# Modulation row: a per-partition scalar multiply on Pool, the partition sum on PE ahead of b_in, and a 24 KB row stored and broadcast back

## The chip, the cores and the metric

The kernel runs on one core of a Trainium2 chip. The metric is the device time of one execution in microseconds; the median of three runs is given. The core has five engines: PE (matmul), DVE and ACT (elementwise work, both read PSUM), Pool (elementwise work in SBUF, and DMA issue), and SP, which here issues the weight loads.

## The reference, cut to what matters

The program is a stack of three transformer blocks at batch 1, 256 tokens, width 1024: a block with differential attention and a dense MLP, a block with a gated recurrence (`hgrn`) and a mixture of experts, and a second network with a modulated block. Only the last one uses the vector that this change is about:

```python
c_act = jax.nn.silu(c)                                   # (1, 1024)
ada = c_act @ w_ada[l] + b_ada[l]                        # (1, 6 * 1024)
shift_a, scale_a, gate_a, shift_m, scale_m, gate_m = jnp.split(ada, 6, axis=-1)
h = modulate(rmsnorm(x, g_mix[l]), shift_a, scale_a)     # h * (1 + scale) + shift
...
x = x + gate_a[:, None, :] * y
```

`ada` depends on `c`, `w_ada` and `b_ada` alone, so it can be computed at any time ahead of the second network. `w_ada` is 1024 x 6144 in float32, 24 MB.

## The kernel before, in words

The stages run one after another, in the order kv_a, kv_b, a_in, diff, a_mem, a_out, dense, b_in, hgrn, b_mem, b_out, route, experts, ada, in_2, gla, moba, out_2, ff_2, final. Every engine has its own instruction list in that order, and semaphores are written out by hand (`wait_ge`, `then_inc`); `at(label)` is the semaphore and count that a labelled instruction sets.

Weight products: SP fills a ring of six 1 MB units (`raw`). For each unit ACT rounds it to a high part (`w_hi`, L787), DVE takes the remainder (`w_lo`, L1183), both with two buffers, and PE forms three products: high by high (L1803), high weight by low activation (L1804), low weight by high activation (L1811). `turn_split` transposes the 256 x 1024 activation on PE (L1828), and ACT (L807) and DVE (L1221) split it into `hT_hi` and `hT_lo`. In `turn_split` and `product` of a stage, each engine works strictly in order.

The modulation vector is built by Pool during dense and b_in, in `ada_sums` (L451 to L488). It keeps six rows of 1024 columns per partition (`acc`, in `work`). For each of the 8 blocks of 128 input rows and each of the 6 parts of 1024 columns, it loads 512 KB of `w_ada` (L465, three buffers, two rows ahead), multiplies it by the column `c_col` (L476), and adds it to `acc` (L479): 48 rounds. After them the partial sums of all 128 partitions, 3 MB, go to DRAM (`ada_parts`, L488), because the buffer `work` is written in stage hgrn. ACT and DVE wait for that store (`ada_stored`, L977 and L1505) ahead of their first instruction of hgrn.

After the experts Pool reads the 3 MB back into `ada` in three DMAs (L736). PE sums over the partitions with a matrix of ones (`ones`, L2171), 12 matmuls of 512 columns, which leaves the sum in all partitions; ACT copies the 12 results back to `ada` (`ada_out`, L921), six ahead of the squares of `norm_2` and six behind them. DVE needs `ada` in `norm` at L1197 (scale) and L1215 (shift), and the gain row `g_mix`, which Pool loads behind the three reads (L689).

In hgrn, PE transposes the outputs of b_in (`turn("hgrn_q", ...)`, L1828), ACT copies them out (L813), DVE clears buffers (L1347) and then runs the recurrence, with Pool's `tree_keys` (L501).

Of the kernel before, what the change touches and what calls it, by code (L numbers as in the profile page):

```python
# [142 lines left out]
def program(nc, A, consts, buckets, out, semaphores, numbers, known, stages, capacity):  # L143
# [17 lines left out]
    with ctx:  # L161
# [16 lines left out]
        c_col = sb("c_col", [P, KC])  # L178
        sumsq = sb("sumsq", [P, TILES])
# [52 lines left out]
        ada_parts = nc.dram_tensor("ada_parts", (P, N_ADA * D), F32, kind="Internal").ap()  # L232
# [47 lines left out]
        def have(name):  # L280
            return name in stages
# [168 lines left out]

        def ada_sums(pool):  # L451
# [16 lines left out]
            def row_block(k, last):  # L468
                for a in range(N_ADA):
# [6 lines left out]
                    pool.tensor_tensor(row, row, c_col[:, k:k + 1].broadcast_to([P, D]), ALU.mult).then_inc(ada_scaled, 1)  # L476
# [10 lines left out]
            pool.wait_ge(ada_ready, N_ADA * (KC + 1))  # L487
            pool.dma_start(ada_parts, work[:, 0:N_ADA * D]).then_inc(ada_stored, 16)  # L488
# [186 lines left out]
        def _(pool):  # L675
# [18 lines left out]
            pool.memset(ones[:, :], 1.0)  # L694
            pool.memset(zero[:, :], 0.0).then_inc(S("zero"), 1)
# [35 lines left out]
            if have("ada"):  # L731
# [3 lines left out]
                for n in range(N_ADA // 2):  # L735
                    pool.dma_start(ada[:, 2 * n:2 * n + 2, :].rearrange("p a d -> p (a d)"),  # L736
                                   ada_parts[:, 2 * n * D:(2 * n + 2) * D]).then_inc(ada_back[n], 16)
# [36 lines left out]
        def _(act):  # L774
# [142 lines left out]
            def ada_out(first, end):  # L917

                for j in range(first, end):
                    act.wait_ge(*at("ada", "summed", j))  # L920
                    act.activation(ada[:, j // 2, j % 2 * 512:(j % 2 + 1) * 512], bank[j % 6][:, :], ACT.Copy)\  # L921
                       .then_inc(S("ada", "out", j), 1)

# [44 lines left out]
            if have("b_in"):  # L968
# [3 lines left out]
                turn_split("norm_b", G["b_in"])  # L972
                product("b_in", proj)
            if have("hgrn"):
                S.stage("hgrn")
                if have("ada"):
                    act.wait_ge(ada_stored, 16)  # L977
# [113 lines left out]
            if have("ada"):  # L1091
                S.stage("ada")
                norm("norm_final", x, mix, at("experts done"))
                ada_out(0, 6)
            if have("in_2"):
                norm("norm_2", x, mix, at("norm_final", "h"))
                ada_out(6, 12)
# [71 lines left out]
        def _(dve):  # L1169
# [332 lines left out]
            if have("hgrn"):  # L1502
                S.stage("hgrn")
                if have("ada"):
                    dve.wait_ge(ada_stored, 16)  # L1505
# [206 lines left out]
            if have("ada"):  # L1712
                S.stage("ada")
                norm("norm_final", x, x, 8)
                dve.wait_ge(*at("ada", "out", 3))
            if have("in_2"):
                S.stage("in_2")
                norm("norm_2", x, mix, 9, 0)
                dve.wait_ge(*at("ada", "out", 11))
# [70 lines left out]
        def _(pe):  # L1790
# [230 lines left out]
            if have("b_in"):  # L2021
                S.stage("b_in")
                turn_split("norm_b", mix, at("norm_b", "h"))
                product("b_in", "norm_b")
# [139 lines left out]
            if have("ada"):  # L2164
                S.stage("ada")
# [117 lines left out]
```

## Time and profile before

| | |
|---|---|
| median of 3 runs | 2169.84 us (2169.73 to 2171.62) |
| span of the profiled execution | 2169.8 us |
| PE busy | 1929.8 us (89%) |
| DVE busy | 1500.8 us (69%) |
| ACT busy | 1140.2 us (53%) |
| Pool busy | 373.6 us (17%) |
| HBM read | 513.72 MB, 239 GB/s over the span |

The profile is of one execution. Its span is the median of the timed runs to within 0.1 us, so times read in it can be set against the median directly. The page gives busy times per engine, the busy share in 40 slices, and the chain of work that ended last: from the last instruction back, at each step to what released it. The trace behind it answers for one stretch, one line or one engine. By the page's slices of 54 us, Pool is busy for 90% or more of the time from about 217 to 488 us.

### The profile page before, as it was taken

Reading aid. Unit: us, or ns where it says so; the run is one execution under the profiler, and the core shown is the slowest. Engines: PE = TensorE matmul, PEld = TensorE weight load, DVE = VectorE, ACT = ScalarE, POOL = GpSimd, SP = SyncE. Lnnn points to the kernel's source line nnn. Section 1 sums busy time; section 2 is a strip of 40 time slices with the busy share of each in tenths; the row PEclk is TensorE's granted clock in tenths of the full one; section 3 lists DMA queues with packets and bytes.
Section 4 is the critical chain, followed back from the end, with each engine's and each line's share of the span. In section 5 each row is a group of like instructions: output and inputs, shape, how many; then the busy total and the mean of one; then the engine's idle time right before and its main releaser. Section 6 shows DMA issues by size and latency. Waiting matters only on the chain.

```text
span 2169.8 us, 27789 instructions
## 1 busy us (share of the span) xinstructions
PE 1929.8 (89%) x9182; PEld 1604.5 (74%) x9182; DVE 1500.8 (69%) x1230; ACT 1140.2 (53%) x1136; POOL 373.6 (17%) x212
## 2 busy tenths in 40 slices
PE   6967899795677999999999999999999798779995
PEld 4856688685666887878788787878878567668894
DVE  4454667573853989879798887988888642645554
ACT  5344334342033767767676676767767553234331
POOL 1005999995400000000000000000000000300000
PEclk9987899897875999999999999999999888679998
DMA  8504678675022999999999999999999843225540
GB/s 290 204 1 144 215 255 259 213 240 177 1 78 64 353 366 320 366 307 365 336 346 369 305 366 312 363 338 343 366 307 367 311 140 116 59 78 173 176 155 20
DMA packets 357365, 518.68 MB, mean 239 GB/s; under 512 B 17106, under 2 KB 286578, under 8 KB 356672
## 3 DMA queue, kind: packets, MB, share of 16 engines
q1 hardware_dynamic: 346736, 476.24, 65.0%
q0 software_dynamic: 10576, 41.76, 5.8%
q8 instruction: 30, 0.49, 0.1%
q14 instruction: 23, 0.19, 0.0%
HBM read 513.72 MB, written 4.21 MB: 239 GB/s over the span
## 4 chain that ended last, share of the span: by engine, by line
PE 69%; POOL 13%; DVE 8%; ACT 4%; issue 4%; DMA 1%; DVEq 0%; ACTq 0%; POOLq 0%
PE bank L1803 20%; PE bank L1811 20%; PE bank L1804 19%; POOL work L479 7%; POOL work L476 6%; PE bank L1878 2%; PE bank L2089 1%; PE bank L1828 1%; DVE w_lo L1183 1%; PE bank L2074 1%; PE bank L1915 1%; ACT w_hi L787 1%; PE bank L1893 1%; PE bank L2050 1%; DVE plain L1372 1%
## 5 line engine op out<-in xcount | busy, mean ns | idle before, releaser
L1183 DVE TENSOR_TENSOR w_lo<-raw,w_hi 128x2048 fp32r<-128x2048 f32 (+1 forms) x454 | 1086.4, 2397 | 190.1 <-ACT w_hi L787 171.2
L787 ACT ACTIVATE w_hi<-raw 128x2048 fp32r<-128x2048 f32 (+1 forms) x454 | 865.9, 1911 | 592.6 <-PE bank L1804 548.8
L1803 PE MATMUL bank<-w_hi,slot_hi 128*128 128x512 f32 x896 | 365.9, 408 | 0.0
L1804 PE MATMUL bank<-w_hi,slot_lo 128*128 128x512 f32 x896 | 354.5, 396 | 0.0
L1803 PE MATMUL bank<-w_hi,hT_hi 128*128 128x512 f32 (+2 forms) x864 | 305.7, 367 | 4.0 <-ACT w_hi L787 4.0
L1804 PE MATMUL bank<-w_hi,hT_lo 128*128 128x512 f32 (+2 forms) x864 | 302.2, 363 | 0.0
L1803 PE MATMUL bank<-w_hi,hid_hi 128*128 128x512 f32 x664 | 261.8, 394 | 6.8 <-DVE hid_lo L1603 4.2
L1804 PE MATMUL bank<-w_hi,hid_lo 128*128 128x512 f32 x664 | 260.2, 392 | 0.0
L1811 PE MATMUL bank<-w_lo,slot_hi 128*128 128x512 f32 x896 | 243.2, 393 | 0.3
L1811 PEld LDWEIGHTS bank<-w_lo,slot_hi 128*128 128x128 f32 x896 | 168.6, 189 | 38.4 <-DVE w_lo L1183 2.4
L1803 PEld LDWEIGHTS bank<-w_hi,slot_hi 128*128 128x128 f32 x896 | 170.7, 191 | 34.0 <-issue 0.3
L1804 PEld LDWEIGHTS bank<-w_hi,slot_lo 128*128 128x128 f32 x896 | 171.2, 191 | 32.8
L1803 PEld LDWEIGHTS bank<-w_hi,hT_hi 128*128 128x128 f32 x864 | 169.9, 197 | 29.3 <-issue 2.9
L1811 PE MATMUL bank<-w_lo,hid_hi 128*128 128x512 f32 x664 | 177.3, 396 | 12.7 <-DVE w_lo L1183 12.7
L1804 PEld LDWEIGHTS bank<-w_hi,hT_lo 128*128 128x128 f32 x864 | 169.5, 196 | 23.8
L736 POOL DMA_DIRECT2D ada<-ada_parts x3 | 1.6, 528 | 1074.1 <-DVE headsq L1711 1074.1
L1811 PE MATMUL bank<-w_lo,hT_hi 128*128 128x512 f32 (+2 forms) x864 | 181.7, 356 | 0.3 <-DVE w_lo L1183 0.3
L1811 PEld LDWEIGHTS bank<-w_lo,hT_hi 128*128 128x128 f32 x864 | 145.4, 192 | 23.5 <-DVE w_lo L1183 1.1
L1811 PEld LDWEIGHTS bank<-w_lo,hid_hi 128*128 128x128 f32 x664 | 124.4, 189 | 41.8 <-DVE w_lo L1183 15.7
L479 POOL TENSOR_TENSOR work<-work 128x1024 f32<-128x1024 f32 x48 | 151.2, 3150 | 4.0
L1803 PEld LDWEIGHTS bank<-w_hi,hid_hi 128*128 128x128 f32 x664 | 124.8, 188 | 35.3 <-issue 3.6
L1804 PEld LDWEIGHTS bank<-w_hi,hid_lo 128*128 128x128 f32 x664 | 124.9, 188 | 26.4
(258 smaller groups left out, 1676.6 us busy)
## 6 DMA issues: line engine op xcount, KB each, us to landing
raw<-in_moe_w_gate_up SPq DMA_DIRECT2D x448, 512.0 KB, 6.1
raw<-in_moe_w_down SPq DMA_DIRECT2D x224, 512.0 KB, 5.5
raw<-in_w_ff SPq DMA_DIRECT2D x64, 512.0 KB, 4.3
work<-in_w_ada POOLq DMA_DIRECT2D x48, 512.0 KB, 4.3
raw<-in_dense_w_gate_up SPq DMA_DIRECT2D x44, 512.0 KB, 5.3
raw<-in_b_w_in SPq DMA_DIRECT2D x24, 512.0 KB, 5.1
raw<-in_w_in SPq DMA_DIRECT2D x24, 512.0 KB, 4.7
raw<-in_dense_w_down SPq DMA_DIRECT2D x22, 512.0 KB, 5.0
```

What stands on the lines that cost most here:

```text
L476: pool.tensor_tensor(row, row, c_col[:, k:k + 1].broadcast_to([P, D]), ALU.mult).then_inc(ada_scaled, 1)
L479: pool.tensor_tensor(acc[:, a, :], acc[:, a, :], row, ALU.add).then_inc(ada_ready, 1)
L787: act.activation(w_hi[:, g % SPLIT, 0:n], raw[:, g % RING, 0:n], ACT.Copy).then_inc(R.hi, 1)
L1183: dve.tensor_tensor(w_lo[:, g % SPLIT, 0:n], raw[:, g % RING, 0:n], f32(w_hi[:, g % SPLIT, 0:n]), ALU.subtract).then_inc(R.lo, 1)
L1372: dve.tensor_tensor(dq, d.q, d.after, ALU.mult).then_inc(S(tag, "queries", level), 1)
L1803: pe.matmul(out_, hi, w_hi[:, s, c:c + w], start=(start and n == 0), stop=False, skip_group_check=True)
L1804: mm = pe.matmul(out_, lo, w_hi[:, s, c:c + w], start=False, stop=False, skip_group_check=True)
L1811: mm = pe.matmul(out_, hi, w_lo[:, s, c:c + w], start=False, stop=(stop and n == len(terms) - 1), skip_group_check=True)
L1828: mm = pe.transpose(bank[6 + j % 2][:, c * P:(c + 1) * P], b, ident)
L1878: mm = pe.matmul(bank[6 + k][:, j * a.dv:(j + 1) * a.dv], a.probsT[k][:, m, s, t * P:(t + 1) * P], a.v(i, m, s), start=(s == 0), stop=(s = ...
L1893: mm = pe.transpose(bank[4 + m][:, s * SEQ + t * P:s * SEQ + (t + 1) * P], a.probs[i % 2][:, m, t, s * P:(s + 1) * P], ident)
L1915: mm = pe.matmul(bank[3 * (level % 2) + n // 4][:, n % 4 * P:(n % 4 + 1) * P], dk[r, h // d.per, c], dq[r, h // d.per, c], start=True, sto ...
```

## The change

Four things change.

- In `row_block`, Pool's multiply becomes `tensor_scalar` with the per-partition scalar `c_col[:, k:k + 1]` where it was `tensor_tensor` with that column broadcast over 1024 elements.
- Ahead of the transposes of b_in, PE waits for the last addition of `ada_sums` and sums the 12 pieces of 512 columns over the partitions: the weights are 12 columns of `one_row`, zero but for the one column that picks the output row, so 12 matmuls accumulate into 12 partitions of `bank[0]`. ACT copies that 12 x 512 block to `work` (`ada_place`) behind its part of `turn_split`, and PE waits for that copy ahead of the product of b_in, which writes the same bank.
- Pool stores this block, 24 KB, in place of the 3 MB, once ACT has copied it. ACT and DVE no longer wait for the store ahead of hgrn.
- After the experts Pool's three reads broadcast the 24 KB to all partitions of `ada`. The 12 matmuls with `ones` and the 12 copies go away; DVE waits for the reads (`ada_back`) itself.

```diff
--- before.py
+++ after.py
@@ -176,6 +176,7 @@
         zero = sb("zero", [P, P], BF16)
         ones = sb("ones", [P, P])
         c_col = sb("c_col", [P, KC])
+        one_row = sb("one_row", [P, 4 * N_ADA - 1])
         sumsq = sb("sumsq", [P, TILES])
         rstd = sb("rstd", [P, TILES])
         top = sb("top", [P, 2, 4])
@@ -229,7 +230,7 @@
         over.close()
 
         bank = [ctx.enter_context(nc.psum_tensor(f"bank{i}", [P, 512], F32)) for i in range(8)]
-        ada_parts = nc.dram_tensor("ada_parts", (P, N_ADA * D), F32, kind="Internal").ap()
+        ada_dram = nc.dram_tensor("ada_dram", (2 * N_ADA, 512), F32, kind="Internal").ap()
         rel_rows = nc.dram_tensor("rel_rows", (2 * MOBA_PAIRS, 2 * SEQ), F32, kind="Internal").ap()
 
 
@@ -448,6 +449,10 @@
         more_loop = ExpertLoop("more")
         ff_loop = Loop("ff")
 
+        def ada_place():
+
+            return work[0:2 * N_ADA, 9216:9728]
+
         def ada_sums(pool):
 
 
@@ -473,7 +478,7 @@
                         load_row(k, ahead)
                     pool.wait_ge(ada_in[a % ADA_BUFFERS], 32 * k + 16 * (a // ADA_BUFFERS + 1))
                     row = rows[:, a % ADA_BUFFERS, :]
-                    pool.tensor_tensor(row, row, c_col[:, k:k + 1].broadcast_to([P, D]), ALU.mult).then_inc(ada_scaled, 1)
+                    pool.tensor_scalar(row, row, c_col[:, k:k + 1], None, ALU.mult).then_inc(ada_scaled, 1)
                     pool.wait_ge(ada_scaled, N_ADA * k + a + 1)
                     pool.wait_ge(ada_ready, N_ADA * k + a + 1)
                     pool.tensor_tensor(acc[:, a, :], acc[:, a, :], row, ALU.add).then_inc(ada_ready, 1)
@@ -484,8 +489,8 @@
             pool.wait_ge(*at("ada", "c"))
             for k in range(KC):
                 row_block(k, k == KC - 1)
-            pool.wait_ge(ada_ready, N_ADA * (KC + 1))
-            pool.dma_start(ada_parts, work[:, 0:N_ADA * D]).then_inc(ada_stored, 16)
+            pool.wait_ge(*at("ada", "row"))
+            pool.dma_start(ada_dram, ada_place()).then_inc(ada_stored, 16)
 
         def tree_keys(pool, S, tag):
 
@@ -692,6 +697,9 @@
             load_gain()
             load_gain()
             pool.memset(ones[:, :], 1.0)
+            pool.memset(one_row[:, 0:2 * N_ADA - 1], 0.0)
+            pool.memset(one_row[:, 2 * N_ADA:], 0.0)
+            pool.memset(one_row[:, 2 * N_ADA - 1:2 * N_ADA], 1.0)
             pool.memset(zero[:, :], 0.0).then_inc(S("zero"), 1)
             if have("a_in"):
                 load_gain()
@@ -734,7 +742,8 @@
                 pool.wait_ge(ada_stored, 16)
                 for n in range(N_ADA // 2):
                     pool.dma_start(ada[:, 2 * n:2 * n + 2, :].rearrange("p a d -> p (a d)"),
-                                   ada_parts[:, 2 * n * D:(2 * n + 2) * D]).then_inc(ada_back[n], 16)
+                                   ada_dram[4 * n:4 * n + 4, :].rearrange("a d -> (a d)").partition_broadcast(P))\
+                        .then_inc(ada_back[n], 16)
                 pool.dma_start(w_gate[:, :], A["w_gla_gate_2"][0]).then_inc(loaded["wgate"], 16)
             if have("in_2"):
                 load_gain()
@@ -913,13 +922,6 @@
                     split_hi(R, g + 5, rounds)
                     silu(1)
                     hidden_hi(1)
-
-            def ada_out(first, end):
-
-                for j in range(first, end):
-                    act.wait_ge(*at("ada", "summed", j))
-                    act.activation(ada[:, j // 2, j % 2 * 512:(j % 2 + 1) * 512], bank[j % 6][:, :], ACT.Copy)\
-                       .then_inc(S("ada", "out", j), 1)
 
             def prepare():
 
@@ -970,11 +972,12 @@
                 begin("b_in")
                 norm("norm_b", x, mix, [at("dense", "added", t) for t in range(TILES)])
                 turn_split("norm_b", G["b_in"])
+                if have("ada"):
+                    act.wait_ge(*at("ada", "summed"))
+                    act.activation(ada_place(), bank[0][0:2 * N_ADA, :], ACT.Copy).then_inc(S("ada", "row"), 1)
                 product("b_in", proj)
             if have("hgrn"):
                 S.stage("hgrn")
-                if have("ada"):
-                    act.wait_ge(ada_stored, 16)
                 turn_copy("hgrn_q", flat(hgrn.q), HG_W * TILES)
 
                 for n in range(HG_W * TILES // 512):
@@ -1091,10 +1094,8 @@
             if have("ada"):
                 S.stage("ada")
                 norm("norm_final", x, mix, at("experts done"))
-                ada_out(0, 6)
             if have("in_2"):
                 norm("norm_2", x, mix, at("norm_final", "h"))
-                ada_out(6, 12)
                 S.stage("in_2")
                 begin("in_2")
                 turn_split("norm_2", G["in_2"])
@@ -1501,8 +1502,6 @@
                 product("b_in", False)
             if have("hgrn"):
                 S.stage("hgrn")
-                if have("ada"):
-                    dve.wait_ge(ada_stored, 16)
                 decayed_start(hgrn)
                 dve.wait_ge(*at("hgrn_f", "taken", 2))
                 low, high = (lb[:, n, :].unsqueeze(2).broadcast_to([P, HG_HEADS, SEQ]) for n in (2, 3))
@@ -1712,11 +1711,12 @@
             if have("ada"):
                 S.stage("ada")
                 norm("norm_final", x, x, 8)
-                dve.wait_ge(*at("ada", "out", 3))
+                dve.wait_ge(ada_back[0], 16)
             if have("in_2"):
                 S.stage("in_2")
                 norm("norm_2", x, mix, 9, 0)
-                dve.wait_ge(*at("ada", "out", 11))
+                for n in (1, 2):
+                    dve.wait_ge(ada_back[n], 16)
                 turn_split("norm_2")
                 product("in_2", False)
                 split_lo(ring, G["in_2"] + 12, 0, KC * GLA_RANK)
@@ -2020,7 +2020,15 @@
                        lambda i: mlp_round(ring, dense_loop, G["dense"] + 3, i, 2 * i + 1, TILES, 2, model_xs))
             if have("b_in"):
                 S.stage("b_in")
+                if have("ada"):
+                    pe.wait_ge(ada_ready, N_ADA * (KC + 1))
+                    for j in range(2 * N_ADA):
+                        mm = pe.matmul(bank[0][0:2 * N_ADA, :], one_row[:, 2 * N_ADA - 1 - j:4 * N_ADA - 1 - j],
+                                       work[:, j * 512:(j + 1) * 512], start=(j == 0), stop=(j == 2 * N_ADA - 1))
+                    mm.then_inc(S("ada", "summed"), 1)
                 turn_split("norm_b", mix, at("norm_b", "h"))
+                if have("ada"):
+                    pe.wait_ge(*at("ada", "row"))
                 product("b_in", "norm_b")
             if have("hgrn"):
                 S.stage("hgrn")
@@ -2161,19 +2169,9 @@
                     pe.sem_inc(more_ring.hi_used, RING)
                     pe.sem_inc(more_ring.used, RING)
                     experts(more_ring, more_loop)
-            if have("ada"):
-                S.stage("ada")
-                pe.wait_ge(*at("experts done"))
-                for j in range(2 * N_ADA):
-                    pe.wait_ge(ada_back[j // 4], 16)
-                    if j >= 6:
-                        pe.wait_ge(*at("ada", "out", j - 6))
-                    pe.matmul(bank[j % 6][:, :], ones[:, :], ada[:, j // 2, j % 2 * 512:(j % 2 + 1) * 512], start=True, stop=True)\
-                      .then_inc(S("ada", "summed", j), 1)
             if have("in_2"):
                 S.stage("in_2")
                 turn_split("norm_2", mix, at("norm_2", "h"))
-                pe.wait_ge(*at("ada", "out", 11))
                 product("in_2", "norm_2")
                 b = B["in_2"] + 6
                 pe.wait_ge(block_out, b - 2)
```

## Rows read from the trace of the kernel before

**Rows 1.** The page's chain that ended last, by engine, share of the span.
```profile
PE 69%; POOL 13%; DVE 8%; ACT 4%; issue 4%; DMA 1%; DVEq 0%; ACTq 0%; POOLq 0%
```

**Rows 2.** Who waited for whom, 500 to 560 us: total us, times, longest us.
```profile
DVE work L1347 <- DMA ada_parts<-work: 22.8, 1, 22.8
ACT work L813 <- DMA ada_parts<-work: 18.2, 1, 18.2
```

**Rows 3.** The chain in order of time, 500 to 545 us: start us, us, what.
```profile
516.79 9.34 DMA ada_parts<-work
...
526.15 0.60 ACT work L813
```

**Rows 4.** Pool in order of time: start us, us, line, operation.
```profile
195.36 1.89 POOL L476 TENSOR_TENSOR work<-work,c_col 128x1024 f32<-128x1024 f32 x1 [1.37 <-DMA work<-in_w_ada]
...
416.30 1.91 POOL L476 TENSOR_TENSOR work<-work,c_col 128x1024 f32<-128x1024 f32 x1
418.29 2.35 POOL L479 TENSOR_TENSOR work<-work 128x1024 f32<-128x1024 f32 x1
...
421.55 1.90 POOL L476 TENSOR_TENSOR work<-work,c_col 128x1024 f32<-128x1024 f32 x1
...
514.15 2.34 POOL L479 TENSOR_TENSOR work<-work 128x1024 f32<-128x1024 f32 x1
```

**Rows 5.** Pool's groups, shapes kept apart: busy us, mean ns | idle before.
```profile
L479 POOL TENSOR_TENSOR work<-work 128x1024 f32<-128x1024 f32 x48 | 151.2, 3150 | 4.0
L476 POOL TENSOR_TENSOR work<-work,c_col 128x1024 f32<-128x1024 f32 x48 | 125.3, 2610 | 2.1 <-DMA work<-in_w_ada 1.4
...
L459 POOL MEMSET work<- 128x1024 f32 x6 | 5.4, 946 | 16.9 <-DVE mix L1298 16.9
```

**Rows 6.** Pool and DVE in order of time, within dense.
```profile
319.56 4.33 POOL L479 TENSOR_TENSOR work<-work 128x1024 f32<-128x1024 f32 x1
...
322.52 3.52 DVE L1183 TENSOR_TENSOR w_lo<-raw,w_hi 128x2048 fp32r<-128x2048 f32 x1 [0.89 <-ACT w_hi L787]
...
324.80 3.00 POOL L476 TENSOR_TENSOR work<-work,c_col 128x1024 f32<-128x1024 f32 x1
```

**Rows 7.** PE in order of time, from the head to the end of b_in.
```profile
429.84 1.97 PE L1828 MATMUL bank<-con,mix 128*128 128x128 f32 x8 [11.35 <-DVE mix L1204]
...
434.05 0.78 PE L1803 MATMUL bank<-w_hi,hT_hi 128*128 128x512 f32 x1
...
507.99 1.10 PE L1828 MATMUL bank<-con,proj 128*128 128x128 f32 x8 [0.75 <-ACT proj L828]
```

**Rows 8.** ACT in order of time, its last split piece ahead of b_in.
```profile
434.43 0.60 ACT L807 ACTIVATE hT_hi<-bank 128x512 fp32r<-128x512 f32 x1 [0.26 <-PE bank L1828]
```

**Rows 9.** Stretches: us, busy PE, PEld, DVE, ACT, POOL, PEclk, DMA, GB/s.
```profile
434.00:440.00 6.00, 6.00 (x20) 4.80 (x19) 5.63 (x4) 0.89 (x3) 5.60 (x4) 0.67 0.37 113
500.00:508.00 8.00, 7.25 (x56) 6.82 (x54) 2.15 (x1) 2.57 (x5) 7.52 (x6) 1.00 0.96 309
```

**Rows 10.** All engines in order of time, after the experts.
```profile
1727.44 1.57 POOL L736 DMA_DIRECT2D ada<-ada_parts  x3 [1074.11 <-DVE headsq L1711]
...
1731.18 2.48 DVE L1204 SCALAR_TENSOR_TENSOR x<-x,rstd,gain 128x1024 f32<-128x1024 f32 x2
1732.88 13.31 PE L2171 MATMUL bank<-ada,ones 128*128 128x512 f32 x24 [9.91 <-DMA ada<-ada_parts]
...
1741.57 1.05 ACT L797 ACTIVATE mix<-x 128x1024 f32<-128x1024 f32 x1
...
1743.93 1.22 DVE L1197 SCALAR_TENSOR_TENSOR ada<-ada,gain 128x1024 f32<-128x1024 f32 x1
...
1747.77 2.36 DVE L1215 TENSOR_TENSOR mix<-mix,ada 128x1024 f32<-128x1024 f32 x2
```

**Rows 11.** The g_mix load: its issue, then size and us to landing.
```profile
1729.50 0.55 POOL L689 DMA_DIRECT2D gain<-in_g_mix  x1
...
gain<-in_g_mix POOLq DMA_DIRECT2D x1, 512.0 KB, 9.6
```

## The prediction

> **What bounds the kernel now.** I read the page's chain first: PE carries 69% of it, but Pool carries 13% [rows 1], though Pool is busy for 17% of the span. So there is a stretch in which the Pool loop that builds the modulation vector is itself the bound. The waits around the end of b_in show where: ACT stands 18.2 us and DVE 22.8 us for the store of `ada_parts` [rows 2]. The chain in order of time puts it together: Pool's last addition starts at 514.15 [rows 4] and ends at 516.5, the 3 MB store takes 9.34 us, and hgrn begins at 526.15 [rows 3]. PE had begun hgrn's transposes at 507.99 [rows 7]. The first four of them are half of 1.10 us, and ACT could have copied them out at about 508.7. So 17.5 us lie between what b_in allows and what Pool and its store allow. This is the gain on offer at this place. From 434.05 to 507.99 [rows 7] PE is at work on the product of b_in; that stretch is PE's, not Pool's.
>
> **The sum goes by one time, P, at which Pool finishes its last addition.** Before, P is 516.5, and nothing on PE depends on it: PE starts b_in at 429.84 [rows 7]. After, PE waits for P ahead of b_in. Everything of b_in is queued behind that wait: PE's transposes, hence ACT's and DVE's halves of `turn_split`, which wait for them in order, and the weight splits behind these; the ring then fills and SP stops too. So the store leaves the path behind P (9.3 us), and the whole of b_in, some 80 us, moves from beside Pool to behind P. That is worth it only if P comes down to about where PE wants to start.
>
> **How far P comes down.** A round without disturbance takes 421.55 less 416.30, 5.25 us: 1.91 for the multiply, 2.35 for the addition, and 0.99 of issue, descriptors and small gaps [rows 4]. Over the 48 rounds the means are 2.61 and 3.15 [rows 5], so a round takes 6.75 us, of which 1.50 is waiting. The rows of both engines show what for [rows 6]: the addition of 319.56 takes 4.33, `w_lo` on DVE, issued during it, takes 3.52 instead of about 2.3 and ends at 326.0, and the multiply of 324.80 takes 3.00 instead of 1.91. They take turns: each stands while the other runs. The Trainium skill (SBUF — State Buffer, "Who interferes with whom") says that a DVE instruction with two SBUF inputs contends with a GpSimd instruction that reads SBUF; the trace agrees (4.33 against 2.35 us), and by it the new multiply, which still reads SBUF, goes on colliding.
>
> The trace has no `tensor_scalar` of this size on Pool. From below, the memset of the same 1024 columns, one stream out and none in, takes 0.946 us [rows 5]; from above, the present multiply takes 1.91 us [rows 4]; nothing excludes that the new form is as slow as that one, and nothing in it is less work than a memset. I take 1.0: with a single full stream in, beside one out, it is nearer to the memset, which has no second operand to fetch. The skill (GPSIMD Engine Reference, "Engine selection") calls one-input operations on GpSimd roughly line-rate; at its 1.2 GHz that is an estimate of 0.85 us, with which the sum below would come out 8 us lower. The same page (§3.1) also gives 1.8 cycles an element as the best of a tight loop, 1.54 us, an estimate with which the sum would be some 25 us higher. No row here decides between them.
>
> With 1.0 a round without waiting is 4.34 us. The waiting I scale with the length of the round, since `w_lo` comes at PE's pace: 1.50 x 5.6 / 6.75 = 1.25, together 5.59. From the first multiply at 195.36 [rows 4] to 429.8 that is 41.9 rounds. From there on PE stands, and DVE with it (its `turn_split` waits for PE), so the other 6.1 rounds take 4.34 us, 26.4 us. The last two rounds load nothing and save the 0.9 us between 420.64 and 421.55 each. P = 429.8 + 26.4 - 1.8 = 454.5, say 455.
>
> **From P to the start of hgrn.** The 12 matmuls: their moving operand has 512 columns of float32, as that of L2171, of which 12 take 13.31 us from an idle PE [rows 10] (two records each). PE will have been idle as there, so I take 13.3. The 12-column weights change nothing that I can price: bounds are 10.3 (all at the late pace) and 20.5 (all at the early pace of 1.71 us). Then the transposes. Before, 4.2 us lay between their start and the product's [rows 7]. Now PE is at full clock, where eight take 1.10 instead of 1.97 us [rows 7]; but PE waits for ACT's copy of the row, and ACT makes it behind its four split pieces. The fourth starts 4.6 us after the first transpose and takes 0.60 [rows 8]; about 1 us less for the faster transposes, one more copy of about 0.65: 4.9 us. Then the product: 434.05 to 508.7 before, 74.65 us, less 1.8 us because the first 6 us ran at a granted clock of 0.67 [rows 9], now full: 72.85. With 0.05 for the semaphore, hgrn starts at P + 91.1. For P = 455 that is 546.1, against 526.15: 19.95 us later.
>
> **After the experts.** Removed are 12 matmuls (13.31 us, of which the first six lie ahead of ACT's squares) and 12 ACT copies. The squares of `norm_2` started at 1741.57 because six copies stood ahead of them; they need only `norm_final`, done at 1733.66 [rows 10]. The next thing is late instead: L1197 needs the gain `g_mix`, issued by Pool behind the three reads at 1729.50 and landed 9.6 us later, 1739.1 [rows 11]. L1197 started at 1743.93 [rows 10], so 4.8 us are gained; 7.8 would be without that load. The broadcast reads write the same 3 MB into SBUF as the reads they replace, so I leave their time as it is; the first is needed at 1736, the others by 1746, and issued at 1727.44 to 1728.5 they fit. If they read slower, the gain of this part is gone: 0 is its other bound. PE starts in_2 from idle both times.
>
> **At nothing:** three memsets of `one_row` at the start (no longer than the 1.0 of a 1024-column one together, and Pool's next load waits for a used gain buffer there); Pool's new wait for the row ahead of its store (behind it only the load of `b_out_norm` and `tree_keys`, both for hgrn, 70 us later); the 24 KB store (needed after the experts). The waits of ACT and DVE ahead of hgrn that disappear are the 9.3 us already counted.
>
> **Sum:** 19.95 - 4.8 = +15.2 us. The span of the profile, 2169.8, is the median to 0.1 us, so 2169.8 + 15.2 = 2185 us. The sum changes sign at P = 439.9, where Pool would have to be 15 us faster than I expect.
>
> **Rivals.**
> - *The multiply gets little or nothing from the new form* (Pool spends its time on something other than the second operand). At 1.91 us a round stays 6.75: 34.7 rounds by 429.8, the other 13.3 at 5.25 less 1.8, P = 498, +58 us, 2228. At 1.4 us P is 474.5, +35, 2204. For it: a column broadcast as second operand already costs 0.44 less than a full one (1.91 against 2.35), so half of it may be gone. Against: the memset's 0.946. Chance of 1.5 us or more: 0.18.
> - *Collisions fall by more than the length of a round*, because a shorter multiply seldom holds DVE back, and so DVE seldom stands in front of the addition. Half the waiting, 0.75 a round: 5.09 us, 46.0 rounds by 429.8, P = 436.5, -3.4 us, 2166.4: no change. Chance 0.12. For it: the 4.33 additions come where DVE was already queued.
> - *Faster: Pool is done before PE needs it.* One mechanism: multiply at the memset's 0.95 and waiting down to a third, 0.5: 4.79 us a round, P = 195.4 + 48 x 4.79 - 1.8 = 423.5, and the 12 matmuls run while PE would be idle for `norm_b` (it is idle for 11.35 us there [rows 7]). The path then has the matmuls' last part only: hgrn some 10 us earlier, and 4.8 behind: -15, 2155. It decides at P under 435.5. Against it: the addition alone, which stays, waits 0.8 a round. Chance 0.08.
> - My own case, P from 444 (0.95 us, 1.0 of waiting) to 476: 2174 to 2206. Chance 0.62.
>
> A difference of 0.2%, 4.3 us, is about what a measurement of this kernel can tell from none. Faster by more: 0.08; within: 0.12; slower by more: 0.80. The range leaves out the faster case, half of the unchanged one, and the multiply above 1.6 us: 2168 to 2216.
>
> **What would show it.** In the changed profile: the mean of the new multiply (1.0, with collisions 1.5) and of the addition (3.0); Pool's last addition at 455; a wait of PE of about 36 us for Pool ahead of the 12 matmuls, at a granted clock of 0.5 at first; no wait of ACT or DVE for a store at hgrn; hgrn's first copy at 546; a DVE wait for the DMA of `g_mix` at L1197. Wrong would be a Pool that ends before 440, or a b_in product that is more than 3 us off 72.

## The result and the profile after

The changed kernel takes 2268.74 us (median; 2267.57 to 2269.20) against 2169.78 before: ratio 1.0446, 95% interval 1.0431 to 1.0462. The direction was forecast, the size was not: 2185 was expected, with 2216 as the upper end.

The head of the page, after:

```profile
span 2265.8 us, 27773 instructions
...
PE 1942.2 (86%) x9182; PEld 1597.9 (71%) x9182; DVE 1469.2 (65%) x1230; ACT 1133.8 (50%) x1125; POOL 378.7 (17%) x215
...
PE 70%; POOL 13%; DVE 8%; issue 4%; ACT 3%; DMA 1%; DVEq 0%; ACTq 0%; POOLq 0%
```

The shares of the chain hardly differ from [rows 1]: Pool is on it for 13% both times, though of a longer span. Pool's two groups over the whole execution (busy us, mean ns | idle before), and then single instructions late in the loop (start us, us):

```profile
L481 POOL TENSOR_SCALAR work<-work,c_col 128x1024 f32<-128x1024 f32 x48 | 155.9, 3249 | 3.2 <-DMA work<-in_w_ada 1.4
L484 POOL TENSOR_TENSOR work<-work 128x1024 f32<-128x1024 f32 x48 | 124.8, 2601 | 4.3
```

```profile
481.66 2.85 POOL L481 TENSOR_SCALAR work<-work,c_col 128x1024 f32<-128x1024 f32 x1
484.60 2.33 POOL L484 TENSOR_TENSOR work<-work 128x1024 f32<-128x1024 f32 x1
...
487.88 2.85 POOL L481 TENSOR_SCALAR work<-work,c_col 128x1024 f32<-128x1024 f32 x1
...
519.93 2.34 POOL L484 TENSOR_TENSOR work<-work 128x1024 f32<-128x1024 f32 x1
```

The new multiply takes 2.85 us undisturbed, where the old one took 1.91 [rows 4] and I had taken 1.0. A round beside an idle DVE takes 6.22 us (487.88 less 481.66). Pool ends at 522.3, 5.8 us later than before, and PE now waits for it. Who waited for whom between 400 and 680 us (total us, times, longest us), and PE and ACT behind that wait (start us, us):

```profile
ACT hT_hi L816 <- PE bank L1828: 110.9, 2, 110.0
DVE hT_lo L1222 <- ACT hT_hi L816: 108.6, 2, 107.8
...
PE bank L2026 <- POOL work L484: 101.8, 1, 101.8
```

```profile
522.32 13.01 PE L2026 MATMUL bank<-work,one_row 128*12 128x512 f32 x24 [101.80 <-POOL work L484]
535.26 1.09 PE L1828 MATMUL bank<-con,mix 128*128 128x128 f32 x8
...
539.17 0.57 ACT L977 ACTIVATE work<-bank 12x512 f32<-12x512 f32 x1
...
612.55 1.08 ACT L822 ACTIVATE work<-bank 128x512 f32<-128x512 f32 x2 [0.75 <-PE bank L1828]
```

The last line is hgrn's first copy, which came at 526.15 before [rows 3]. The two waits for the store [rows 2] are gone, and a wait of 101.8 us of PE has come instead. After the experts (DVE, start us, us):

```profile
1834.35 0.17 DVE L1194 TENSOR_SCALAR sumsq<-sumsq 128x2 f32<-128x2 f32 x1 [2.32 <-ACT mix L806]
1837.19 1.22 DVE L1198 SCALAR_TENSOR_TENSOR ada<-ada,gain 128x1024 f32<-128x1024 f32 x1 [2.67 <-DMA gain<-in_g_mix]
```

This is the wait for the gain row. From the end of the experts (`headsq`, 1727.07 before and 1825.44 after) to PE's first transpose of in_2 it is 23.1 us before and 18.0 after.

The two profiled spans differ by 96.0 us. They divide at two marks into 86.4 us up to hgrn's first copy (612.55 less 526.15), 12.0 us from there to the end of the experts (1212.9 against 1200.9), and -2.4 us behind it (440.4 against 442.7). The second part was in no step of the prediction. The medians differ by 99.0 us. In every other run here the time of the profiled execution is 1.8 us above its span, so that of before is the one timed at 2171.62, and that its span equals the median is a coincidence.

### The profile page after: what moved, and what is told of

Same layout as the page of the kernel before. It is cut to its first block, busy times and chain, and to the rows that moved or that the text cites. A ratio compares the mean times of both kernels' runs of the same rounds, so it can differ in the third digit from the quotient of the medians.

```text
span 2265.8 us, 27773 instructions
## 1 busy us (share of the span) xinstructions
PE 1942.2 (86%) x9182; PEld 1597.9 (71%) x9182; DVE 1469.2 (65%) x1230; ACT 1133.8 (50%) x1125; POOL 378.7 (17%) x215
## 4 chain that ended last, share of the span: by engine, by line
PE 70%; POOL 13%; DVE 8%; issue 4%; ACT 3%; DMA 1%; DVEq 0%; ACTq 0%; POOLq 0%
PE bank L1803 20%; PE bank L1804 20%; PE bank L1811 20%; POOL work L481 7%; POOL work L484 6%; PE bank L1828 1%; PE bank L2097 1%; PE bank L1878 1%; PE bank L2082 1%; DVE w_lo L1184 1%; PE bank L1915 1%; PE bank L2058 1%; PE bank L2026 1%; PE bank L1893 1%; DVE top L1275 1%
## 5 line engine op out<-in xcount | busy, mean ns | idle before, releaser
L1184 DVE TENSOR_TENSOR w_lo<-raw,w_hi 128x2048 fp32r<-128x2048 f32 (+1 forms) x454 | 1055.8, 2329 | 221.5 <-ACT w_hi L796 208.9
L481 POOL TENSOR_SCALAR work<-work,c_col 128x1024 f32<-128x1024 f32 x48 | 155.9, 3249 | 3.2 <-DMA work<-in_w_ada 1.4
```

What stands on the lines that cost most here:

```text
L481: pool.tensor_scalar(row, row, c_col[:, k:k + 1], None, ALU.mult).then_inc(ada_scaled, 1)
L1184: dve.tensor_tensor(w_lo[:, g % SPLIT, 0:n], raw[:, g % RING, 0:n], f32(w_hi[:, g % SPLIT, 0:n]), ALU.subtract).then_inc(R.lo, 1)
```

## The experiments

Two questions: is the first part the price of the multiply and the place of the wait, and nothing else; and where do the 12 us come from. Each ratio is against the kernel before on the same chip. Where a time has no ratio with it, it is of one run; 17 runs of before on one chip took 2165.26 to 2175.52 us, so a single time tells little below 5 us, and the rows of the trace tell more.

**The multiply alone, the arrangement alone.** In `ts_only` the kernel before gets the new multiply; in `tt_multiply` the changed kernel gets the old one back. The lines are those of `tt_multiply`; `ts_only` has them the other way round.

```diff
-                    pool.tensor_scalar(row, row, c_col[:, k:k + 1], None, ALU.mult)
+                    pool.tensor_tensor(row, row, c_col[:, k:k + 1].broadcast_to([P, D]), ALU.mult)
```

> The kernel before with nothing changed but the multiply, which becomes the one with a per-partition scalar. Theory: it takes 2.85 us undisturbed wherever it stands, 0.94 more than the old form, and waits less (0.96 us a round against 1.5 in dense), so a round takes about 7.15 us: Pool ends at 195.4 + 48 x 7.15 - 1.8 = 537, the store lands at 546.5, 20 us later than before: 2190 us. Rival: its 2.85 us belong to the changed kernel only (place of the buffers, or Pool running alone); then it takes no more than 1.91 here and the time is 2170 or less.

> The changed kernel with the multiply of before (column broadcast, two operands); all else as changed. Theory: of the loss, what is due to the multiply's form goes, and what is due to PE waiting ahead of b_in stays. A multiply alone takes 1.91 us again, 35 rounds are done by 429.8 us as before, the other 13 run beside an idle DVE at 5.25 us less 1.8: Pool ends at about 497.5. hgrn's first copy comes 90.3 us behind that, as it does in the changed kernel (522.3 to 612.6), so at 588, 61.6 us later than before, and 5.1 us are gained after the experts: 2226 us. Rival: the multiply's form is not what costs; then Pool ends near 522 again and the time stays near 2268.

`ts_only` took 2191.02 us, ratio 1.0105 (1.0075 to 1.0136), as expected. One multiply in it beside an idle DVE, the waits between 400 and 680 us, and hgrn's first copy:

```profile
514.88 2.85 POOL L476 TENSOR_SCALAR work<-work,c_col 128x1024 f32<-128x1024 f32 x1
```

```profile
DVE work L1347 <- DMA ada_parts<-work: 44.3, 1, 44.3
...
ACT work L813 <- DMA ada_parts<-work: 38.9, 1, 38.9
```

```profile
546.54 1.09 ACT L813 ACTIVATE work<-bank 128x512 f32<-128x512 f32 x2 [38.88 <-DMA ada_parts<-work]
```

So the multiply costs the same 2.85 us in either kernel, and here Pool ends at 536.8 and hgrn starts 20.4 us later than before. `tt_multiply` took 2245.53 us, 1.035 (1.0327 to 1.0372). hgrn's first copy was expected at 588:

```profile
588.76 1.08 ACT L822 ACTIVATE work<-bank 128x512 f32<-128x512 f32 x2 [0.75 <-PE bank L1828]
```

Pool ends at 498.9. The arrangement with the old multiply, that is PE's wait for Pool ahead of b_in less the store that it saves, costs 62.6 us at this mark. The time on the whole missed its expectation by 19 us, because the 12 us are in this kernel too (1212.5 us from that copy to the end of the experts). Of the rest, 4.9 us lie behind the experts, 0.8 ahead of hgrn, and 1.8 are the step from a span to a time.

**What the new multiply is made of.** `ts_imm` has the number 1.0 where the column stood; `ts_512` multiplies only half the columns.

```diff
-                    pool.tensor_scalar(row, row, c_col[:, k:k + 1], None, ALU.mult)
+                    pool.tensor_scalar(row, row, 1.0, None, ALU.mult)                                   # ts_imm
+                    pool.tensor_scalar(row[:, 0:512], row[:, 0:512], c_col[:, k:k + 1], None, ALU.mult) # ts_512
```

> The changed kernel with the immediate 1.0 as the scalar in place of the column (the factor c is left out of the modulation vector, nothing else). It asks what the 2.85 us are made of. If they come from fetching the scalar of each partition, the multiply falls to about 1.0 us, Pool ends at about 455 and the time is about 2185, the blind sum with its own price. If they belong to the form itself, the multiply stays at 2.85 and the time near 2268.

> The changed kernel with the new multiply on the first 512 of each 1024 columns only (the other half of each row is added unscaled). It gives the slope of the new multiply. Theory: 2.85 us for 1024 columns is nearly all per column, 2.7 ns each, with 0.1 fixed, so 512 take 1.45 us. Rival: the form has a fixed cost of about 1.9 us above a line-rate multiply; then 512 columns take about 2.4 us. With 1.45 us a round is 4.8 us undisturbed, Pool ends near 478, and the time is about 2268.7 - 44 = 2225; with 2.4 us near 2248.

They took 2266.45 and 2230.49 us, one run each; the second is 5 us above its expectation. One multiply of each, beside an idle DVE:

```profile
512.16 2.77 POOL L481 TENSOR_SCALAR work<-work 128x1024 f32<-128x1024 f32 x1
```

```profile
452.11 1.57 POOL L481 TENSOR_SCALAR work<-work,c_col 128x512 f32<-128x512 f32 x1
```

The column as scalar, in place of a number, is 0.08 us of it. Between 512 and 1024 columns the time goes from 1.57 to 2.85: 2.5 ns a column, and by that slope 0.29 us fixed (1.45 us was expected for 512). The form itself is slow per column on Pool: 2.5 ns, where the two-operand multiply with a broadcast column takes 1.91 us for 1024, under 1.9 ns a column. Why it is so, no run shows.

**What the arrangement gives when Pool is early.**

```diff
-            for k in range(KC):
-                row_block(k, k == KC - 1)
+            for k in range(KC // 2):
+                row_block(k, k == KC // 2 - 1)
...
-                    pe.wait_ge(ada_ready, N_ADA * (KC + 1))
+                    pe.wait_ge(ada_ready, N_ADA * (KC // 2 + 1))
```

It also has the old multiply, as `tt_multiply`.

> The changed kernel with the old multiply and only 4 of the 8 blocks of w_ada (24 of 48 rounds; the other half of the sum is left out), so that Pool is done long before PE reaches b_in. It shows what the arrangement gives when its condition holds. Theory: Pool ends at 195.4 + 24 x 6.75 - 1.8 = 356; the 12 matmuls run while PE waits for norm_b and end at 432; hgrn's first copy comes at about 511 where it came at 526, and 5.1 us are gained after the experts; with the 12 us lost in between as in the others, 2161 us. Rival: the wait ahead of b_in costs for another reason than Pool's lateness; then hgrn starts later than 526 here too.

It took 2167.64 us in one run. PE and ACT in it:

```profile
422.66 10.47 PE L2026 MATMUL bank<-work,one_row 128*12 128x512 f32 x24
433.06 1.09 PE L1828 MATMUL bank<-con,mix 128*128 128x128 f32 x8
```

```profile
511.81 1.09 ACT L822 ACTIVATE work<-bank 128x512 f32<-128x512 f32 x2 [0.74 <-PE bank L1828]
```

With Pool done in time (at 360.0), PE does not wait, and hgrn starts 14.3 us earlier than before, 0.8 us from what was expected. The 12 matmuls take 10.47 us here against 13.01: the granted clock is 1.00 from 420 to 435 us in this run, and 0.80 over the 13 us of the matmuls in the changed kernel. The whole time is 6.6 us above its expectation; 3.1 of them lie behind the experts (440.7 us, where 437.6 were expected), 1.8 are the step from span to time.

**The sum behind b_in.** The old multiply, and the wait moved to where `work` is needed. Not shown: the sum ahead of b_in goes away, ACT's copy of the row moves behind the product, and DVE waits for the sum ahead of hgrn.

```diff
                 turn_split("norm_b", mix, at("norm_b", "h"))
-                if have("ada"):
-                    pe.wait_ge(*at("ada", "row"))
                 product("b_in", "norm_b")
             if have("hgrn"):
...
+                    pe.wait_ge(*all_in)
+                    for j in range(2 * N_ADA):
+                        pe.wait_ge(ada_ready, N_ADA * KC + j // 2 + 1)
+                        mm = pe.matmul(bank[0][0:2 * N_ADA, :], one_row[:, 2 * N_ADA - 1 - j:4 * N_ADA - 1 - j],
...
```

> The old multiply, and the sum over the partitions moved from ahead of b_in to behind its product: each of the 12 matmuls waits only for its own part of the vector, and ACT and DVE wait for the sum ahead of hgrn. Theory: it is the place of the wait that costs, so b_in is beside Pool again, Pool ends at 516.5 as before, ten of the matmuls run beside Pool's last rounds, two behind it (3.4 us at the low clock), then the 12-partition copy: hgrn's first copy at 521.3, 5 us earlier than before, and 5.1 us are gained after the experts: 2160 us. Rival: the matmuls or the 12-partition copy cost more than the 9.3 us store they replace, wherever they stand; then hgrn starts later than 526 and the time is 2165 or more.

It took 2177.64 us, 1.0043 (1.0031 to 1.0056): neither 2160 nor a gain. But hgrn's first copy came early enough:

```profile
512.40 10.47 PE L2034 MATMUL bank<-work,one_row 128*12 128x512 f32 x24 [0.75 <-ACT proj L837]
...
522.80 1.10 PE L1830 MATMUL bank<-con,proj 128*128 128x128 f32 x8
```

The copy is at 523.5, 2.65 us earlier than before. Pool ended at 519.4 and was not the limit. The matmuls were: they run in a row behind the product, where I had expected ten of them beside Pool's last rounds. The loss is again behind that mark: 1212.8 us to the end of the experts, against 1200.9 before.

**The 12 us.** The cast of `pickT` happens once in each of the eight experts, so its first and last start bound seven steps. In before the first step takes 151.6 us and the other six 127.8 to 129.0. This view of one tile (durations ns min/median/max, first and last start us) for before, after, `late_sum`, and `ts_only`:

```profile
L1636 DVE CAST pickT<-staged x8: 279/286/295, 694.9 to 1618.2; 128x256 fp32r<-128x256 f32 x8
```

```profile
L1635 DVE CAST pickT<-staged x8: 282/284/293, 780.8 to 1714.4; 128x256 fp32r<-128x256 f32 x8
```

```profile
L1637 DVE CAST pickT<-staged x8: 280/282/294, 691.1 to 1624.8; 128x256 fp32r<-128x256 f32 x8
```

```profile
L1636 DVE CAST pickT<-staged x8: 279/282/294, 717.7 to 1640.9; 128x256 fp32r<-128x256 f32 x8
```

Seven steps take 923.3, 933.6, 933.7 and 923.2 us. The kernels with `one_row` are 10 us slower here, though the experts' code is the same. `one_row` is a new buffer ahead of the large ones (`proj`, `work`, `hid`, `slot`): 23 columns, 92 bytes a partition, which I take as rounded up to 96. `raw`, `w_hi`, `w_lo`, `hT_hi` and `hT_lo` are allocated ahead of it and do not move. Eight kernels vary that alone:

```diff
+        one_row = sb("one_row", [P, 4 * N_ADA - 1])   # row_only: the kernel before, buffer and memsets, unused
+        one_row = sb("one_row", [P, 32])              # row_32; 16, 64, 128 columns in row_16, row_64, row_128
-        one_row = sb("one_row", [P, 4 * N_ADA - 1])   # the kernels with PE's sum:
+        one_row = sb("one_row", [P, 64])              # late_sum_64, after_64
```

> The kernel before with only the 23-column buffer one_row added behind c_col, and its three memsets; nobody reads it. In the changed kernel and in both variants with PE's sum, an expert takes 129.7 us where it takes 128.6 before and in the kernel with the new multiply alone, and the whole stretch from hgrn's first copy to the end of the experts is 12 us longer. Theory A: the 92 bytes a partition move every later buffer (slot_hi, hid_hi, proj and so on) off a 64-byte boundary, and PE's matmuls from them get 1% slower; then this kernel shows 129.7 us an expert and some 10 us on the whole, 2179. Theory B: it is the altered instruction list of PE (its loops lie at other places in memory); then this kernel is like before, 128.6 us an expert, 2168.

> The kernel with the sum behind b_in's product, with one_row 64 columns wide (256 bytes a partition) instead of 23 (92 bytes), which leaves the later buffers at the same place modulo 64 bytes as before. Theory A (buffer places): an expert takes 128.6 us again and the 12 us go: 2177.6 - 12 = 2166, under the kernel before. Theory B (PE's instruction list): an expert stays at 129.7 and the time near 2177.

> The changed kernel with one_row 64 columns wide instead of 23, nothing else. It splits the loss of 99 us into its two causes. Theory: the wait ahead of b_in stays as it is (Pool ends at about 522, hgrn's first copy near 612.6), and the 12 us of buffers off a 64-byte boundary go: an expert takes 128.6 us, the whole 2268.7 - 12 = 2257. Rival: the 12 us came with the late start of the stages, and stay: 2268.

> The control for row_only: the kernel before with the same unused buffer and memsets, but 32 columns (128 bytes a partition), which moves the later buffers by two times 64 bytes. Theory: it is the place modulo 64 bytes that costs, so this kernel is as before, an expert 128.6 us, ratio 1.000. Rival: any shift, or the memsets, cost; then it is at 1.0067 as row_only.

> The kernel before with an unused buffer of 64 columns (256 bytes a partition) behind c_col and its three memsets. Theory (place of the later buffers modulo 256 bytes): as before, 128.6 us an expert, ratio 1.000. Rival (the memsets or the altered Pool list): 129.8 us and 1.007, as with 23 and 32 columns.

> The same with 128 columns (512 bytes). Theory: 128.6 us an expert, as before. Rival (only one particular place is fast): 129.8.

> The same with 16 columns (64 bytes). Theory: 129.8 us an expert and some 12 us on the whole, since 64 is no multiple of 256. Rival (the place modulo 64 matters after all, and row_32 was slow for another reason): 128.6.

> The kernel before with two unused buffers of 32 columns, one behind c_col and one ahead of proj: the small buffers in between (sumsq to flag) move by 128 bytes, proj, work, hid, slot and all behind them by 256. Theory: the large ones, from which PE reads its weights in dense and experts, have to keep their place, so 128.6 us an expert. Rival: the small ones do, and it stays at 129.8.

I take the large buffers to begin at byte 158784 of a partition before, which is 64 modulo 256. No view of a run shows an address, so the third column rests on that; the shifts in the second do not. Steps from the same view as above, of one profiled execution each:

| kernel | shift, bytes | place modulo 256 | seven steps, us | ratio (interval), or one run |
|---|---|---|---|---|
| before | 0 | 64 | 923.3 | |
| row_64 | 256 | 64 | 923.5 | 1.0003 (0.9988 to 1.0019) |
| row_128 | 512 | 64 | 923.4 | 2169.51 us |
| row_small | 256 (small ones 128) | 64 | 923.4 | 2174.11 us |
| late_sum_64 | 256 | 64 | 923.6 | 0.9958 (0.9940 to 0.9976) |
| after_64 | 256 | 64 | 921.1 | 1.0368 (1.0350 to 1.0385) |
| row_16 | 64 | 128 | 917.0 | 2166.22 us |
| row_only | 96 | 160 | 933.6 | 1.0067 (1.0044 to 1.0090) |
| row_32 | 128 | 192 | 933.8 | 1.0071 (1.0057 to 1.0086) |

`row_only` and `late_sum_64` settled that the place of the buffers is the cause and not PE's instruction list: an unused buffer brings the loss, and 256 bytes instead of 96 take it away. My first rule, modulo 64 bytes, fell with `row_32`: its buffers are at a multiple of 64 and it is slow. Modulo 256 fits the nine. `row_16` missed its expectation: 64 bytes of shift are not slow but faster than before. In `row_small` the small buffers move by 128 bytes and the large ones by 256, and its steps are those of before: the place of the large ones matters, and the shift of the small ones costs nothing. `after_64` gained more than expected: its first copy of hgrn comes at 617.7 (612.6 was expected, Pool ends at 527.0), but 1198.6 us lie from there to the end of the experts and 433.8 behind them, where the changed kernel has 1212.9 and 440.4.

What is slower is each matmul that reads a moved buffer. In dense, the streamed operand `w_hi` is the same for two kinds of matmuls: those that load `hT_hi` and `hT_lo` as their other operand (LDWEIGHTS), which did not move, and those that load `hid_hi` and `hid_lo`, which did. The first and last start of a run of both kinds, in `row_32` and then in before (start us, us):

```profile
301.81 0.39 PE L1808 MATMUL bank<-w_hi,hT_lo 128*128 128x512 f32 x1
...
305.01 0.39 PE L1808 MATMUL bank<-w_hi,hT_lo 128*128 128x512 f32 x1
...
307.05 0.40 PE L1807 MATMUL bank<-w_hi,hid_hi 128*128 128x512 f32 x1
...
310.55 0.40 PE L1808 MATMUL bank<-w_hi,hid_lo 128*128 128x512 f32 x1
```

```profile
300.04 0.40 PE L1804 MATMUL bank<-w_hi,hT_lo 128*128 128x512 f32 x1
...
303.26 0.39 PE L1804 MATMUL bank<-w_hi,hT_lo 128*128 128x512 f32 x1
...
305.30 0.39 PE L1803 MATMUL bank<-w_hi,hid_hi 128*128 128x512 f32 x1
...
308.73 0.40 PE L1804 MATMUL bank<-w_hi,hid_lo 128*128 128x512 f32 x1
```

These are 14 and 15 steps: 229 ns from start to start with `hT` and 233 with `hid` in `row_32`, 230 and 229 in before. Over the whole execution, the median from one start to the next behind a matmul of `w_hi` with `hT_hi` is 227 ns in all of these kernels. With `hid_hi` it is 229 in before, 227 in `row_16`, 232 in `row_only` and 236 in `row_32`. In the last six of the seven steps PE is busy for 98% of the time (758.83 of 771.7 us in before, 764.08 of 779.0 in `row_32`), so a per cent of its work is a per cent of the time.

**A version that beats both.** `late_sum_64` with the load of `g_mix` ahead of the three reads, and then the same with two other places of the large buffers:

```diff
                 load_gain()
+                if have("in_2"):
+                    load_gain()
                 pool.wait_ge(*at("experts done"))
```

> late_sum_64 with the load of the gain row g_mix issued before the three reads of the modulation row instead of behind them. Theory: in the changed kernel the scale step of norm_2 waits for that load (landed at 1837.2, where the squares were done at about 1834.5); with it away the first read becomes the limit or the squares do, and 2.7 us are gained against late_sum_64. Rival: the first read of the row lands no earlier than the gain did, and nothing is gained.

> late_gain_64 with one_row 80 columns wide (320 bytes), so that the large buffers begin at 128 modulo 256 where they began at 64. Theory: 127.8 us an expert as in row_16, 6.5 us less over the seven steps between experts, and 7 us on the whole: about 0.988 of before where late_gain_64 has 0.991. Rival: the gain of row_16 belonged to that kernel; then 128.6 and 0.991.

> The same with 48 columns (192 bytes), so that the large buffers begin at a multiple of 256 bytes. Theory: this is the natural boundary and at least as good as 128, so 127.8 us an expert or less, 0.988. Rival: the pace does not follow the boundary; then anything up to 129.9 us an expert and 0.997.

`late_gain_64` took 2155.27 us, 0.9911 (0.9883 to 0.9939). From the end of the experts to L1198 it is 9.0 us, with the squares as the limit:

```profile
1732.20 0.17 DVE L1194 TENSOR_SCALAR sumsq<-sumsq 128x2 f32<-128x2 f32 x1 [2.33 <-ACT mix L806]
1732.27 1.22 DVE L1198 SCALAR_TENSOR_TENSOR ada<-ada,gain 128x1024 f32<-128x1024 f32 x1
```

In `late_sum_64` it was 11.7 us, with a wait of 2.58 us for the gain: 2.7 us as expected. `late_gain_80` (place 128) took 2148.48 us, 0.9898 (0.9881 to 0.9916), with 919.7 us for the seven steps; its interval overlaps that of `late_gain_64`, so the steps show the better place and the whole time does not. `late_gain_48` (place 0) had 930.5 us for the seven steps and a ratio of 0.9995 (0.9982 to 1.0007): the multiple of 256 bytes is not the good place. Its profiled execution, 2163.02 us, is the fastest of its 12 runs (2163.02 to 2174.26).

## Why the prediction was right or wrong

**What bounds the kernel, and the sum by P: right.** The blind sum said that hgrn's first copy comes at P + 91.1. It came at P + 90.3 in the changed kernel, P + 89.9 with the old multiply. The parts held too: the 12 matmuls 13.01 us against 13.3, the product of b_in 72.75 us (539.80 to 612.55) against 72.85, a granted clock of 0.52 while PE waits for Pool (421 to 522 us), no wait for a store at hgrn.

**The price of the multiply: wrong, and most of the miss.** I put it between the memset's 0.946 and the old multiply's 1.91 us, took 1.0, and named nothing that would make it slower than the form that it replaces. It takes 2.85. The upper end was no bound: a row of another form says what that form costs, not that the new one can't cost more, and that the new form has one operand less to fetch was an argument about the work, not about how Pool does it. With 2.85 and the waiting left at 1.25, the same steps give 31.5 rounds by 429.8 and 16.5 more at 6.19, less 1.8: P = 530, 75 us above the forecast. With the measured waiting they give what was measured: 33 rounds by 429.8, 15 more at 6.22, less 1.8, is 521.3 against 522.3. So the price of the multiply put P 75 us off, and the smaller waiting took 8 us back. The Trainium skill (GPSIMD Engine Reference, "Engine selection") has one-input operations on GpSimd at roughly line-rate. This case's trace disagrees, with 2.5 ns a column for this one, which at the 1.2 GHz of that page is an estimate of three cycles; the measurement decides.

**The waiting of a round: wrong in size, to the other side.** I scaled it to 1.25 us. In the changed kernel it was 0.96 up to 429.8 (means of 3.43 and 2.72 us against 2.85 and 2.34 undisturbed), with a longer round. The rival that collisions fall with a shorter multiply had its reason wrong as well: the waiting fell, from 1.55 in the same stretch of before, with a longer one.

**The rivals.** "The multiply gets little or nothing from the new form" was the right kind of rival, at a chance of 0.18 and a price of 58 us, cut off at the old duration; beyond it lay what happened. The faster and the unchanged rival need P under 440. `half_rounds` shows that the mechanism of the faster one is real (hgrn 14.3 us earlier once Pool is early), and `tt_multiply` (P at 498.9), beside the changed kernel, that neither form of multiply reaches it.

**After the experts: right.** 4.8 us expected, 5.1 measured, and the gain row was the next limit, as the 2.7 us of `late_gain_64` confirm.

**Not foreseen: 12 us.** "At nothing" I had put three memsets of `one_row`. What counted was the buffer itself, which moves everything behind it: `after_64` takes 2251.46 us where the changed kernel takes 2268.74, ratios 1.0368 and 1.0446. Together, on the profiled spans: 15.2 forecast, 67.3 for P, -0.8 for P to hgrn, -0.3 behind the experts, 12.0 from hgrn to the end of the experts and 2.7 in the stages after in_2 begins, 96.1 of 96.0. In `after_64` both of the last two stretches are shorter, by 14.3 and 6.6 us.

## What to carry to other kernels

Where a change swaps one form of an instruction for another on an engine that the trace doesn't show it on, no other form's row bounds it from above: measure it, or give the range an end well above what it replaces. Before moving a wait ahead of a long stage, work out by which time its source has to be done, and prefer the latest place that the data allow: here, with the old multiply, the same sum started hgrn 2.65 us earlier behind b_in and 62.6 us later ahead of it. And after adding a buffer, compare the pace of a stage that was not touched; if it has changed, pad the buffer.

## What the runs showed of the hardware

- Pool's `tensor_scalar` in float32 takes 2.85 us for 128 x 1024 and 1.57 for 128 x 512, with a number as scalar 2.77; the two-operand multiply with a column broadcast takes 1.91, the two-operand addition 2.34.
- Against DVE's two-operand `w_lo` the new multiply behaves otherwise than the old. In the changed kernel (Pool, then DVE, start us, us):

```profile
302.42 2.85 POOL L481 TENSOR_SCALAR work<-work,c_col 128x1024 f32<-128x1024 f32 x1
305.37 2.59 POOL L484 TENSOR_TENSOR work<-work 128x1024 f32<-128x1024 f32 x1
```

```profile
302.60 3.10 DVE L1184 TENSOR_TENSOR w_lo<-raw,w_hi 128x2048 fp32r<-128x2048 f32 x1
```

`w_lo` needs 2.29 us alone. Had it stood until the multiply ended at 305.27, it would have ended at 307.6; it ended at 305.70. So most of it ran beside this multiply, which lost nothing, where the old pair took turns [rows 6]. That holds where the multiply starts first; where `w_lo` has started well before it, the multiply takes longer (6.04 us at 234.71), and over the first 33 its mean is 3.43.
- The place in SBUF of the buffers from which PE loads the operand that it holds (LDWEIGHTS), modulo 256 bytes, sets the pace of its matmuls by up to 4% (median 227 to 236 ns from start to start) and the time of the experts by up to 2%: 128 is best (917.0 to 919.7 us for the seven steps), 64 next (921.1 to 923.6), then 0 (930.5), 160 and 192 (933.6 to 933.8). The buffers of the streamed operand did not move in any of these kernels, and matmuls that load `hT_hi` kept 227 ns in all of them. ACT and DVE write the moved buffers too, and no run parts the writing from the loading, or moved the buffers one by one; why the place counts stays open.
